# First turn of the attention heads in another order on four engines, and the forget gate's sums made one pair of products further back

## The chip, the cores and the metric

The program runs on one core of one Trainium2 chip. The metric is the device time of one execution in microseconds (us). A profiled execution gives a trace in which every instruction of every engine has its place; the times below are read from one such execution.

## The reference, cut to what matters

A decoder trunk of two layers works on 528 tokens (16 learned meta tokens and 512 of the input), 1024 channels, in float32. Layer 0 mixes tokens with eight stick-breaking heads and eight forgetting heads side by side. The change touches only that mixer:

```
proj  = h @ w_in                       # q, k, v of 8 stick-breaking and 8 forgetting heads, and 8 forget logits
log_f = log_sigmoid(f_logit + b_f);  c = cumsum(log_f)          # over the tokens
z   = qa @ ka.T * scale                # stick-breaking: weights from a reversed cumulative sum of log_sigmoid(-z)
a_w = exp(log_sigmoid(z) + rest);      out_sb  = a_w @ va
s   = qb @ kb.T * scale + c[q] - c[k]  # forgetting: causal softmax
out_fox = softmax(s) @ vb
h   = h + concat(out_sb, out_fox) @ w_out
```

The rest is RMS norms, four SwiGLU feed-forward halves (1024 to 2816 and back) and, in layer 1, a pooling mixer.

## The kernel before, in words

**Precision and products.** Every float32 operand is split into a high part (rounded by ScalarE, "hi") and a low part (the difference, made by VectorE, "lo"), and a product is three matmul passes: hi·hi, lo·hi, hi·lo. Large products are made two strips at a time, in *pairs*, with seven half-size block products in place of eight (a Strassen-like scheme). Each block product is 12 matmuls of 128x264. So each pair needs, on VectorE, sums of weight blocks (L2213, L2219, L2224), low parts of weights (`s23_low` L2240, `s14_low` L2245, `a_low` L2229, `a22_low` L2234) and four drains of results (L1338, L1345, L1352, L1359) with a scaling pass (L1365).

**The input projection.** 24 strips of 128 columns: four are made plainly, and 20 in ten pairs whose first strip `p.f` is 4, 6, ..., 22. Strips below `QK` = 16 are queries and keys; they are split and stored to DRAM (`qk_dram`), from which the heads are staged. Strips 16 to 23 are values and stay in SBUF (`v_rows`). The program of a pair on TensorE (`qkv_pe`) is: product 1; third product of the pair before; product 2; product 6 (waits for `s23_low` of this pair); fourth product of the pair before; product 7; product 5 (waits for `s14_low` of this pair). Then comes the next pair, whose first product waits for its `a_low`. In the last pair (`p.f` = 22) TensorE has extra work between: `first_turned_values` (transposes 0 and 1 of the values) ahead of product 6, and `first_scores` (scores of head step 0 and 1, transposes 2 and 3) ahead of product 7.

**Forget gate.** `fg`, `fg_abs`, `fg_sum`, `fg_one` are four rows of `fg_room`, which lies in the same SBUF as `q_all[0]` (three rows: the queries of head 0 of a pair of heads) and `fx_kk[0]` (the fourth row: forgetting keys). At the end of pair 16 VectorE makes the log-sigmoid (L1436) and its cumulative sum (a scan, L1438). ScalarE copies the high parts (L1195, L1196) in pair 18, VectorE makes the low parts at that pair's end (L1441, L1442; they raise `c_low`), GpSimd stores them to DRAM (L3294, raises `c_stored`), and they are read back as two small transfers of two rows into `fx_qc` and `fx_kc`.

**Staging (`stage_heads`, SyncE's DMA queue, a program written out by hand).** For the first head: four transfers of keys; wait for `c_low`; six of queries and forgetting queries into `q_all`, two of forgetting keys into `fx_kk`; wait for `c_stored`; two small ones of the sums; then `fetch_out(0..3)`, the first four strips of the output projection's weights (512 KB each, and each waits until the raw buffer is free). All fourteen transfers of head 0 count on one semaphore, `staged[0]`, and TensorE's first score (L885, `stick_scores(0, 0)`) waits for the whole of it. Later come head 1 and the values (L784, L788) into `head_v`.

**The heads' turns.** Eight steps (two heads of four tiles) per pair of heads, four pairs of heads. TensorE makes stick-breaking scores (L885, L891), forgetting scores (L903), sticks (L923, L927, L930), transposes of probabilities (L943), and values (L968 and on; L988). ScalarE makes |z|, exp, log (L1113, L1120, L1126), the softmax's exp (L1142), the softplus's high part (`act_split`, L1152) and the weights (L1161). VectorE masks (L1452), makes softplus (L1462), the running stick (L1477), the probabilities (L1514) and the low part of softplus (L1518, raises `sp_low`). GpSimd masks (L3307). The first turn (`hp` = 0) overlaps the end of the projection: value strips 22 and 23 are drained by `c21_out` and `bottom_scaled` (L1359, L1365) between steps, and eleven pieces of transposed values go out of PSUM (`v_turned_out`, L1155 on ScalarE, L731 on VectorE). In the first turn TensorE's forgetting scores of step 3 wait for `c21_out` of the last pair, transposes 8 and 9 for `bottom_scaled`, transpose 10 for copy 7, and the first product with values (`stick_values(0, 0)`, L968) for copy 9, for the GpSimd transfer of the first head's values (L3345, semaphore `v_first`), and for the zeroed half of `head_v[0]` (`v_zero`).

Of the kernel before, what the change touches and what calls it, by code (L numbers as in the profile page):

```python
# [30 lines left out]
ALU = mybir.AluOpType  # L31
AXX = mybir.AxisListType.X

P = 128
# [10 lines left out]
QKV, QKV_PLAIN = 24, 4  # L45
QK = 16
# [4 lines left out]
HD = 64  # L51
NH = 8
# [109 lines left out]
def trunk(nc, x, meta_tokens, g_ffn1, w_ffn1_in, w_ffn1_out, g_mix, g_ffn2, w_ffn2_in, w_ffn2_out,  # L162
# [5 lines left out]
    with ctx:  # L168
# [123 lines left out]

        fg, fg_abs, fg_sum, fg_one = (fg_room[0:NH, i, :] for i in range(4))
        fg_both, fg_low = fg_room[:, 0, :], fg_room[LOW_ROW:, 0, :]
# [449 lines left out]
        def stage_heads(sp, ph, fetch_out):  # L744
# [36 lines left out]
            def stage_v(hp, e, kinds, landed_v):  # L781
                for kind in kinds:
                    tiles = slice(0, QT - kind)
                    sp.dma_start(head_v[e][:, kind, tiles, HD * e:HD * (e + 1)],  # L784
                                 v_tok[:, kind, tiles, bass.ds((2 * hp + e) * HD, HD)]).then_inc(landed_v, 16)
                if e == 1 and 1 in kinds:
                    for a in range(2):
                        sp.dma_start(head_v[1][META * a:META * (a + 1), 1, QT - 1, HD * a:HD * (a + 1)],  # L788
                                     v_tok[0:META, 1, QT - 1, bass.ds((2 * hp + a) * HD, HD)]).then_inc(staged_v[e], 16)
# [4 lines left out]
            sp.wait_ge(aug_ones, 3)  # L794
            stage_keys(0, 0)
            sp.wait_ge(c_low, 2)
            stage_queries(0, 0)
            stage_forgetting(0, 0)
            sp.wait_ge(c_stored, 16)
            stage_sums(0, 0)  # L800
            for j in range(4):
                fetch_out(j)
            sp.wait_ge(p5_done, ph.pairs[-1].s + 1)
# [10 lines left out]
            sp.wait_ge(v_first, 16)  # L814
            sp.wait_ge(v_zero, 3)
            stage_v(0, 1, (0, 1), staged_v[1])
# [257 lines left out]
        def attn_act(act, ph, split, tail, root, a_high, s23_high, s14_high, a22_high, p1_copy, u2_copy, u4_copy, X, A):  # L1074
# [111 lines left out]
            for p in ph.pairs:  # L1186
# [3 lines left out]
                if prev is not None:  # L1190
                    p1_copy(ph, p, two)
                    s14_high(p, prev)
                    if prev.f == QK:
                        act.wait_ge(fg_step, 5)
                        nc.scalar.activation(c_parts[:, 0, :], fg_sum, ACT.Copy).then_inc(c_high, 1)  # L1195
                        nc.scalar.activation(c_parts[:, 2, :], fg_sum, ACT.Copy, scale=-1.0).then_inc(c_high, 1)  # L1196
                    top_high(prev)
                    if nxt is not None:
                        a_high(nxt)
                    else:  # L1200
                        nc.scalar.preload_act_table_set("natural_log_exp_and_others")
                        act.wait_ge(s14_lo, p.s + 1)
                        v_turned_out(act, 0, copy)
                    u2_copy(ph, p, two)
# [22 lines left out]
            def act_step(hp, g, first):  # L1227
# [3 lines left out]
                if first and g == 2:  # L1231
                    act_log(hp, 2)
                    act_probs(hp, 2)
                    v_turned_out(act, 6, copy)
                    act_split(hp, 2)
                    v_turned_out(act, 7, copy)
                    return
# [48 lines left out]
        def attn_dve(dve, ph, split, tail, inverse, clear_sums, weight_sums_13, weight_sum_2, weight_sum_4, a_low, a22_low,  # L1286
# [111 lines left out]
            for p in ph.pairs:  # L1398
# [17 lines left out]
                if prev is not None:  # L1416
                    s14_low(p)
                    if prev.f < QK:
                        qk_low(prev.f)
                if prev is not None and nxt is not None:  # L1420
                    a_low(nxt)
# [9 lines left out]
                if nxt is not None:  # L1431
                    a22_low(nxt)
                if p.f == QK:
                    dve.wait_ge(fg_act, 3)
# [3 lines left out]
                    nc.vector.tensor_tensor_scan(fg_sum, fg_one, fg, 0.0, ALU.mult, ALU.add).then_inc(fg_step, 1)  # L1438
                elif p.f == QK + 2:
                    dve.wait_ge(c_high, 2)  # L1440
                    nc.vector.tensor_tensor(c_parts[:, 1, :], fg_sum, c_parts[:, 0, :], ALU.subtract).then_inc(c_low, 1)  # L1441
                    nc.vector.tensor_tensor(c_parts[:, 3, :], c_parts[:, 0, :], fg_sum, ALU.subtract).then_inc(c_low, 1)  # L1442

# [36 lines left out]
            def dve_step(hp, g, first):  # L1480
# [3 lines left out]
                if first and g == 2:  # L1484
                    dve_mask(hp, 2)
                    dve_softplus(hp, 2)
                    c21_out(last_p)
                    bottom_scaled(last_p)
# [1753 lines left out]
        def _(pool):  # L3242
# [14 lines left out]
            for ph in PHASES:  # L3257
# [81 lines left out]
                weight_mask(0, 0)  # L3339
                weight_mask(0, 1)  # L3340
                wait_v_copy(pool, 3)
                wait_v_copy(pool, QT - 1)
                pool.wait_ge(v_first, 16)
                pool.wait_ge(unit_done, ph.n0 + QKV)
                pool.dma_start(head_v[0][:, 0, 0:QT, 0:HD], v_tok[:, 0, 0:QT, 0:HD]).then_inc(v_first, 16)  # L3345
                softplus_mask(0, 2)
                for e in range(2):
                    nc.gpsimd.memset(head_v[e][:, :, :, HD * (1 - e):HD * (2 - e)], 0.0).then_inc(v_zero, 1)
                    pool.wait_ge(v_zero, e + 1)
                nc.gpsimd.memset(head_v[1][:, 1, QT - 1, HD:2 * HD], 0.0).then_inc(v_zero, 1)  # L3350
# [53 lines left out]
```

## Time and profile before

| | us |
|---|---|
| median of 3 runs (lowest, highest) | 1757.29 (1756.66, 1757.46) |
| the profiled execution's own time | 1756.96 |
| its span in the trace | 1755.2 |
| TensorE busy | 1739.5 (99%) |
| VectorE busy | 1401.1 (80%) |
| ScalarE busy | 939.0 (53%) |
| GpSimd busy | 71.8 (4%) |
| granted TensorE clock | 1.0 of full speed throughout |

The span is the stretch from the first to the last instruction; the execution's own time is 1.8 us longer. Times in the rows count from the span's start. The input projection's pairs lie at about 390 to 510 us, the first turn of the heads at 498 to 529 us, the other three turns up to 616 us.

### The profile page before, as it was taken

The page shows a single profiled execution, that of the slowest core. Times are in us where ns is not written, and L with a number is a line of the kernel's source. Part 1 is how long each engine was busy: PE and PEld are TensorE (multiplying, and loading weights), DVE is VectorE, ACT ScalarE, POOL GpSimd, SP SyncE. Part 2 cuts the span into 40 slices and gives each one's busy share as a digit, 9 for nine tenths or more (in the row PEclk, how much of TensorE's full clock was granted, in tenths as well). Part 3 has the DMA queues.
Part 4 walks back from the last instruction along what each step waited for, and adds up shares of the span by engine and source line. Part 5 has one row for each costly group of instructions (what it writes and reads, how often), then busy time and mean ns, then how long its engine had stood idle before and what let it go on. Part 6 is the DMA issues. An engine that isn't in the chain of part 4 may idle for free.

```text
span 1755.2 us, 34355 instructions
## 1 busy us (share of the span) xinstructions
PE 1739.5 (99%) x13600; PEld 1693.1 (96%) x13600; DVE 1401.1 (80%) x2018; ACT 939.0 (53%) x1554; POOL 71.8 (4%) x193
## 2 busy tenths in 40 slices
PE   8999999999999999999999999999999999999998
PEld 8999999999998899999999999999999988899997
DVE  6856998789988858848998688489987788499875
ACT  6433655555578844625655546246555445266555
POOL 0000000002122202000000000000000000000000
PEclk9999999999999999999999999999999999999999
DMA  5243333236655332333343323333342323343332
GB/s 159 85 121 97 97 108 110 80 103 197 196 157 149 88 109 85 97 97 97 97 119 92 102 87 108 97 96 97 97 113 74 91 77 104 89 114 110 97 95 74
DMA packets 334087, 187.01 MB, mean 107 GB/s; under 512 B 17713, under 2 KB 324593, under 8 KB 333937
## 3 DMA queue, kind: packets, MB, share of 16 engines
q1 hardware_dynamic: 330144, 175.31, 35.6%
q0 software_dynamic: 2960, 8.98, 1.4%
q8 instruction: 106, 1.74, 0.4%
q10 hardware_dynamic: 832, 0.62, 0.1%
q14 instruction: 45, 0.36, 0.1%
HBM read 171.58 MB, written 10.88 MB: 104 GB/s over the span
## 4 chain that ended last, share of the span: by engine, by line
PE 88%; DVE 8%; issue 2%; ACT 1%; DMA 1%; POOL 0%; DVEq 0%; ACTq 0%; SPq 0%; POOLq 0%
PE pair L2820 50%; PE pair L2792 18%; PE pair L2761 8%; PE pair L3156 4%; PE pair L2807 1%; PE pair L968 1%; PE pair L988 1%; PE pair L3032 1%; PE pair L2998 1%; DVE sums_w L2213 1%; DVE w_lo L2245 1%; DVE w_lo L2240 1%; DVE qk_lo L1319 1%; PE pair L903 0%; PE pair L885 0%
## 5 line engine op out<-in xcount | busy, mean ns | idle before, releaser
L2820 PE MATMUL pair<-b_hi,w_hi 128*128 128x264 f32 (+1 forms) x1464 | 415.9, 284 | 0.0
L2820 PE MATMUL pair<-b_lo,w_hi 128*128 128x264 f32 (+1 forms) x1464 | 415.0, 283 | 0.0
L2820 PE MATMUL pair<-b_hi,w_lo 128*128 128x264 f32 (+1 forms) x1464 | 414.6, 283 | 0.0
L2820 PEld LDWEIGHTS pair<-b_hi,w_hi 128*128 128x128 f32 x1464 | 275.7, 188 | 0.9 <-issue 0.5
L2820 PEld LDWEIGHTS pair<-b_hi,w_lo 128*128 128x128 f32 x1464 | 275.7, 188 | 0.0
L2820 PEld LDWEIGHTS pair<-b_lo,w_hi 128*128 128x128 f32 x1464 | 275.6, 188 | 0.0
L1738 ACT ACTIVATE w_hi<-sums_w 128x1024 fp32r<-128x1024 f32 x188 | 198.6, 1057 | 104.7 <-PE pair L2820 60.9
L1738 ACT ACTIVATE w_hi<-raw_all 128x1024 fp32r<-128x1024 f32 (+1 forms) x188 | 158.9, 845 | 141.9 <-PE pair L2820 101.2
L2820 PE MATMUL pair<-blocks_hi,w_hi 128*128 128x264 f32 (+1 forms) x816 | 231.3, 283 | 0.3 <-ACT parts L1925 0.3
L2820 PE MATMUL pair<-blocks_lo,w_hi 128*128 128x264 f32 (+1 forms) x816 | 231.5, 284 | 0.0
L2820 PE MATMUL pair<-blocks_hi,w_lo 128*128 128x264 f32 (+1 forms) x816 | 230.8, 283 | 0.0
L2792 PE MATMUL pair<-b_hi,w_lo 128*128 128x264 f32 (+1 forms) x766 | 173.8, 298 | 0.0
L2792 PE MATMUL pair<-b_hi,w_hi 128*128 128x264 f32 (+1 forms) x766 | 173.5, 298 | 0.0
L2792 PE MATMUL pair<-b_lo,w_hi 128*128 128x264 f32 (+1 forms) x766 | 173.4, 298 | 0.0
L2131 DVE TENSOR_TENSOR w_lo<-raw_all,w_hi 128x1024 fp32r<-128x1024 f32 x117 | 142.6, 1221 | 28.2 <-ACT w_hi L1709 28.2
L1709 ACT ACTIVATE w_hi<-raw_all 128x1024 fp32r<-128x1024 f32 x117 | 121.7, 1050 | 63.3 <-PE pair L2792 58.8
L2820 PEld LDWEIGHTS pair<-blocks_hi,w_hi 128*128 128x128 f32 x816 | 153.8, 188 | 0.7 <-ACT parts L1925 0.5
L2820 PEld LDWEIGHTS pair<-blocks_hi,w_lo 128*128 128x128 f32 x816 | 153.7, 188 | 0.0
L2820 PEld LDWEIGHTS pair<-blocks_lo,w_hi 128*128 128x128 f32 x816 | 153.5, 188 | 0.2
L2240 DVE TENSOR_TENSOR w_lo<-sums_w,w_hi 128x1024 fp32r<-128x1024 f32 x94 | 114.8, 1221 | 24.0 <-ACT w_hi L1738 24.0
L2637 DVE SCALAR_TENSOR_TENSOR h<-pair,h 128x528 f32<-128x528 f32 (+1 forms) x61 | 42.9, 703 | 109.0 <-PE pair L2792 108.4
L2245 DVE TENSOR_TENSOR w_lo<-sums_w,w_hi 128x1024 fp32r<-128x1024 f32 x94 | 114.6, 1219 | 17.8 <-ACT w_hi L1738 17.6
(355 smaller groups left out, 3788.1 us busy)
## 6 DMA issues: line engine op xcount, KB each, us to landing
raw_all<-in_w_ffn_in SPq DMA_DIRECT2D x173, 512.0 KB, 4.0
raw_all<-in_w_ffn_out SPq DMA_DIRECT2D x64, 512.0 KB, 4.4
raw_all<-in_w_ffn_out SPq DMA_DIRECT2D x32, 384.0 KB, 3.7
raw_all<-in_w_attn_in SPq DMA_DIRECT2D x24, 512.0 KB, 4.7
q_all<-qk_dram SPq DMA_DIRECT2D x48, 132.0 KB
qk_dram<-qk_hi POOLq DMA_DIRECT2D x16, 264.0 KB, 4.5
qk_dram<-qk_lo POOLq DMA_DIRECT2D x16, 264.0 KB, 3.0
raw_all<-in_w_attn_out SPq DMA_DIRECT2D x8, 512.0 KB, 4.9
```

The costliest lines, as they stand in the source:

```text
L968: mm = nc.tensor.matmul(o_main[:, 0, q0 - META:SEQ], head_v[e][:, 0, 3 - s, :], w[:, 0:nq], start=(g == 0), stop=True, skip_group_check=True)
L988: mm = nc.tensor.matmul(own, head_v[e][:, 1, b, :], turned_p[s][:, b, :], start=(g == 0 and b == 0), stop=True, skip_group_check=True)
L1709: nc.scalar.activation(w_hi[j][:, :], raw[j][:, :], ACT.Copy).then_inc(hi_ready, 1)
L1738: return nc.scalar.activation(dst, src, ACT.Copy)
L2131: nc.vector.tensor_tensor(w_lo[j][:, :], raw[j][:, :], w_hi[j][:, :], ALU.subtract).then_inc(lo_ready, 1)
L2240: nc.vector.tensor_tensor(w_lo[1][:, :], S23, w_hi[1][:, :], ALU.subtract).then_inc(s23_lo, 1)
L2245: nc.vector.tensor_tensor(w_lo[2][:, :], s14(p.q), w_hi[2][:, :], ALU.subtract).then_inc(s14_lo, 1)
L2637: nc.vector.scalar_tensor_tensor(hm, pair_of(OUT_BANK[m], ph.last), 0.5, hm, ALU.mult, ALU.add).then_inc(drained, 1)
L2761: mm = nc.tensor.matmul(psum[j][:, bank, c0:c0 + cols], w[j][:, blk], rhs[v][:, k, t0:t0 + cols], start=(k == 0 and w is w_hi and v == 0), ...
L2792: mm = nc.tensor.matmul(bank_of[:, bank, c0:c0 + cols], w[slot][:, blk], rhs[v][:, k, from_:from_ + cols], start=(k == 0 and w is w_hi and ...
L2820: mm = nc.tensor.matmul(dst, w[slot][:, c0 + kk * P:c0 + (kk + 1) * P], rhs(v, kk), start=(fresh and kk == 0 and w is w_hi and v == 0), st ...
L3156: mm = nc.tensor.matmul(psum[j][:, bank, c0:c0 + cols], w[j][:, blk], X[v][:, k, t0:t0 + cols], start=(k == 0 and w is w_hi and v == 0), s ...
```

## The change

It moves work; no arithmetic is added or removed.

- Forget gate: log-sigmoid and scan move from the end of pair 16 to the end of pair 18, the high parts on ScalarE from pair 18 to pair 20, the low parts on VectorE from the end of pair 18 to the middle of pair 20, after `s14_low` and ahead of `a_low` of the last pair. `fg_sum` changes places with `fg_one`, so that it lies under `fx_kk[0]`.
- SyncE's queue: queries and forgetting queries wait for the scan only (`fg_step` 5), forgetting keys for `c_low`; `fetch_out(0..3)` comes ahead of the sums. The wait for `v_zero` 3 stands only ahead of the two small transfers of meta values.
- VectorE: in step 2 of the first turn `c21_out` comes ahead of `softplus`.
- ScalarE: in step 2 copy 7 comes ahead of `act_split`.
- GpSimd: `head_v[0]` is zeroed first, then the mask of step 2's softplus, then the transfer of the first head's values; `head_v[1]` is zeroed only once `sp_low` is 3, that is after VectorE's L1518 of step 2.

```diff
-        fg, fg_abs, fg_sum, fg_one = (fg_room[0:NH, i, :] for i in range(4))
+        fg, fg_abs, fg_one, fg_sum = (fg_room[0:NH, i, :] for i in range(4))
...
                 if e == 1 and 1 in kinds:
+                    if isinstance(hp, int) and hp == 0:
+                        sp.wait_ge(v_zero, 3)
                     for a in range(2):
...
             stage_keys(0, 0)
+            sp.wait_ge(fg_step, 5)
+            stage_queries(0, 0)
+            put(0, fx_qq[0][0:HD, :], part(0, 0, 8))
+            put(0, fx_qq[0][HD:P, :], part(0, 1, 8))
             sp.wait_ge(c_low, 2)
-            stage_queries(0, 0)
-            stage_forgetting(0, 0)
+            put(0, fx_kk[0][0:HD, :], part(0, 0, 12))
+            put(0, fx_kk[0][HD:P, :], part(0, 0, 12))
+            for j in range(4):
+                fetch_out(j)
             sp.wait_ge(c_stored, 16)
             stage_sums(0, 0)
-            for j in range(4):
-                fetch_out(j)
...
             sp.wait_ge(v_first, 16)
-            sp.wait_ge(v_zero, 3)
             stage_v(0, 1, (0, 1), staged_v[1])
...
-                    if prev.f == QK:
+                    if prev.f == QK + 2:
                         act.wait_ge(fg_step, 5)
...
                     v_turned_out(act, 6, copy)
+                    v_turned_out(act, 7, copy)
                     act_split(hp, 2)
-                    v_turned_out(act, 7, copy)
...
                     s14_low(p)
                     if prev.f < QK:
                         qk_low(prev.f)
+                    if p.f == QK + 4:
+                        dve.wait_ge(c_high, 2)
+                        (the two low parts, c_low)
...
-                if p.f == QK:
+                if p.f == QK + 2:
                     (log-sigmoid and scan)
-                elif p.f == QK + 2:
-                    (the two low parts, c_low)
...
                     dve_mask(hp, 2)
+                    c21_out(last_p)
                     dve_softplus(hp, 2)
-                    c21_out(last_p)
                     bottom_scaled(last_p)
...
                 weight_mask(0, 1)
+                pool.wait_ge(unit_done, ph.n0 + QKV)
+                nc.gpsimd.memset(head_v[0][:, :, :, HD:2 * HD], 0.0).then_inc(v_zero, 1)
+                pool.wait_ge(v_zero, 1)
+                softplus_mask(0, 2)
                 wait_v_copy(pool, 3)
                 wait_v_copy(pool, QT - 1)
                 pool.wait_ge(v_first, 16)
-                pool.wait_ge(unit_done, ph.n0 + QKV)
                 pool.dma_start(head_v[0][:, 0, 0:QT, 0:HD], v_tok[:, 0, 0:QT, 0:HD]).then_inc(v_first, 16)
-                softplus_mask(0, 2)
-                for e in range(2):
-                    nc.gpsimd.memset(head_v[e][:, :, :, HD * (1 - e):HD * (2 - e)], 0.0).then_inc(v_zero, 1)
-                    pool.wait_ge(v_zero, e + 1)
+                pool.wait_ge(sp_low, 3)
+                nc.gpsimd.memset(head_v[1][:, :, :, 0:HD], 0.0).then_inc(v_zero, 1)
+                pool.wait_ge(v_zero, 2)
```

## Rows read from the trace of the kernel before

**Rows 1.** The page: busy time of each engine, share of the span, instructions.
```profile
PE 1739.5 (99%) x13600; PEld 1693.1 (96%) x13600; DVE 1401.1 (80%) x2018; ACT 939.0 (53%) x1554; POOL 71.8 (4%) x193
```
**Rows 2.** Timeline of TensorE in the last pairs (start, length, line, idle before and releaser).
```profile
473.02 0.51 PE L2820 MATMUL pair<-qkv_t,w_hi 128*128 128x264 f32 x2 [0.44 <-DVE w_lo L2240]
...
477.98 0.53 PE L2820 MATMUL pair<-qkv_t,w_hi 128*128 128x264 f32 x2 [0.32 <-DVE w_lo L2245]
...
489.75 0.28 PE L2820 MATMUL pair<-b_hi,w_hi 128*128 128x264 f32 x1
...
494.14 1.03 PE L872 MATMUL pair<-ident,v_rows 128*128 128x128 f32 x8
...
497.92 0.34 PE L885 MATMUL pair<-q_all,sb_kk 128*128 128x144 f32 x2
```
**Rows 3.** Timeline of VectorE, pairs 16 to 20.
```profile
469.88 0.69 DVE L1436 SCALAR_TENSOR_TENSOR fg_room<-fg_room 8x528 f32<-8x528 f32 x1
470.61 1.25 DVE L1438 TENSOR_TENSOR_SCAN fg_room<-fg_room 8x528 f32<-8x528 f32 x1
...
481.75 0.69 DVE L1442 TENSOR_TENSOR c_room<-c_room,fg_room 8x528 fp32r<-8x528 f32 x1
...
487.83 1.22 DVE L2229 TENSOR_TENSOR w_lo<-raw_all,w_hi 128x1024 fp32r<-128x1024 f32 x1
```
**Rows 4.** Timeline of SyncE's DMA queue, head 0 and the weights behind it.
```profile
482.47 3.97 SPq L747 DMA_DIRECT2D q_all<-qk_dram  x6
486.48 1.24 SPq L747 DMA_DIRECT2D fx_kk<-qk_dram  x2
...
488.55 4.82 SPq L1621 DMA_DIRECT2D raw_all<-in_w_attn_out  x4
```
**Rows 5.** The tile raw_all from 486 to 500 us: the four weight transfers.
```profile
L1621 SPq DMA_DIRECT2D raw_all<-in_w_attn_out x4: 393/537/1604, 488.5 to 491.8; - x4
...
DMA to landing us min/median/max: 5.0/6.1/6.9
```
**Rows 6.** Busy time by stretch (PE, PEld, DVE, ACT, POOL, clock, DMA share, GB/s).
```profile
497.00:498.00 1.00, 1.00 (x11) 1.00 (x10) 0.00 (x0) 0.06 (x1) 0.00 (x0) 1.00 0.24 70
```
**Rows 7.** Timeline of TensorE at the end of the projection.
```profile
509.40 0.28 PE L2820 MATMUL pair<-qkv_t,w_lo 128*128 128x264 f32 x1
...
510.55 0.45 PE L903 MATMUL pair<-fx_kk,q_all 128*128 128x400 f32 x1 [0.41 <-DVE v_rows L1359]
...
511.56 0.85 PE L872 MATMUL pair<-ident,v_rows 128*128 128x128 f32 x6 [0.20 <-DVE v_rows L1365]
512.68 0.66 PE L872 MATMUL pair<-ident,v_rows 128*128 128x128 f32 x4 [0.28 <-ACT v_tok L1155]
...
514.77 0.48 PE L968 MATMUL pair<-b_rows,head_v 128*128 128x144 f32 x2 [0.28 <-ACT v_tok L1155]
```
**Rows 8.** Timeline of VectorE, step 2 of the first turn.
```profile
509.58 0.57 DVE L1462 SCALAR_TENSOR_TENSOR b_rows<-pair,b_rows 128x400 f32<-128x400 f32 x1 [0.56 <-ACT b_rows L1126]
510.07 0.42 DVE L1359 TENSOR_TENSOR v_rows<-pair,qkv_parts 128x264 f32<-128x264 f32 x1
...
511.76 0.84 DVE L1514 TENSOR_SCALAR b_rows<-b_rows,stats 128x400 f32<-128x400 f32 x1
```
**Rows 9.** Timeline of GpSimd there, and the landing of its transfer (line L3345).
```profile
510.35 0.90 POOL L3345 DMA_DIRECT2D head_v<-v_tok  x1 [2.86 <-DVE b_rows L1462]
511.26 0.54 POOL L3307 TENSOR_SCALAR_AFFINE_SELECT b_rows<-b_rows 128x128 f32<-128x128 f32 x1
...
DMA to landing us min/median/max: 3.9/3.9/3.9
```
**Rows 10.** Timeline of ScalarE there.
```profile
512.27 0.36 ACT L1155 ACTIVATE v_tok<-pair 16x256 f32<-16x256 f32 x1
```
**Rows 11.** DMA issues of the page: transfers like GpSimd's, by SyncE, and the smallest.
```profile
head_v<-v_tok SPq DMA_DIRECT2D x7, 160.0 KB, 2.5
...
head_v<-v_tok SPq DMA_DIRECT2D x8, 4.0 KB, 1.7
```

More of the change, by code:

```diff
@@ L1419, in attn_dve @@
                         qk_low(prev.f)
+                    if p.f == QK + 4:
+                        dve.wait_ge(c_high, 2)
+                        nc.vector.tensor_tensor(c_parts[:, 1, :], fg_sum, c_parts[:, 0, :],
+                                                ALU.subtract).then_inc(c_low, 1)
+                        nc.vector.tensor_tensor(c_parts[:, 3, :], c_parts[:, 0, :], fg_sum,
+                                                ALU.subtract).then_inc(c_low, 1)
                 if prev is not None and nxt is not None:
@@ L1438, in attn_dve @@
                     nc.vector.tensor_tensor_scan(fg_sum, fg_one, fg, 0.0, ALU.mult, ALU.add).then_inc(fg_step, 1)
-                elif p.f == QK + 2:
-                    dve.wait_ge(c_high, 2)
-                    nc.vector.tensor_tensor(c_parts[:, 1, :], fg_sum, c_parts[:, 0, :], ALU.subtract).then_inc(c_low, 1)
-                    nc.vector.tensor_tensor(c_parts[:, 3, :], c_parts[:, 0, :], fg_sum, ALU.subtract).then_inc(c_low, 1)
             def dve_mask(hp, g):
```

## Prediction, made before the changed kernel was run

> **What bounds the kernel now.** The page's first part comes first: TensorE is busy for 99% of the span, no other engine above 80% [rows 1]. So only time in which TensorE stands still can be won, and every delay of TensorE is paid in full. Next I read TensorE's own timeline around the forget gate and the first turn, looking for the few brackets with idle time, and for matmuls that start later than their pitch (the 12 matmuls of a product take 1.46 us where nothing is awaited). There are two places. In pair 18, products 6 and 5 each wait for VectorE's low parts. Between their starts lie 36 matmuls, which take 4.39 us unhindered (489.75 to 494.14) and took 4.96 here, so the second wait cost 0.57, 0.25 more than its bracket, which counts from a modelled end; some 0.1 of that is the restart itself. For the first, 0.44 in its bracket, I take 0.6 and for the second 0.5 [rows 2]. Behind the projection come four more: 0.41, 0.20, 0.28 and 0.28 us [rows 7]. From 515 us on TensorE has almost no gap until the heads are done, so a shift made before that point reaches the end. All that stands still here is 1.1 + 1.17 = 2.3 us, or 0.13% of the time; a measurement of this kernel can tell 0.2% (3.5 us) from no change. That alone says "within 0.2%" unless a new wait comes in.
>
> **Part 1, the forget gate's sums.** On VectorE the same instructions run between 469.88 and the end of pair 20, without idle time in either order. Before, log-sigmoid and scan (469.88 to 471.78, 1.90 us) stand ahead of pair 18's low parts [rows 3]. After, these come 1.90 us earlier: neither 0.6 nor 0.5 is left. TensorE runs 1.1 us ahead. But scan and low parts (two of 0.69, pitch 0.62) [rows 3] now all lie in pair 20 and just before it, ahead of `a_low` of the last pair. The list ahead of that `a_low` is the same as before, so it still ends at 487.83 + 1.22 = 489.05 [rows 3]. TensorE would want it at 489.75 - 1.1 = 488.65 [rows 2] and gets it at about 489.10. A new stall of 0.45 us takes part back: **-0.65 us** is left at this point. Low parts of the last pair's product 6 end where they did, and TensorE needs them only behind transposes 0 and 1 (494.14) [rows 2]; ScalarE's two copies go into gaps. Both cost nothing; without these gaps they would cost their 1.2 us.
>
> **Part 2, SyncE's queue.** TensorE would now reach the first score at 497.92 - 0.65 = 497.27 [rows 2]. Before, it found all fourteen transfers landed. After, `c_low` comes at 487.9 instead of 482.44 (its L1442 ended there) [rows 3], as the low parts now end where `a_low` starts. The six transfers that no longer wait for it gain nothing, since they were early. The two of forgetting keys go out at 487.9 instead of 486.48, the first weights at 487.9 + 1.24 = 489.15 instead of 488.55 [rows 4]: +0.6. The third and fourth weights still wait for the last pair's low parts (the fourth goes out at 491.8) [rows 5]. The two small transfers of sums now follow all four, issued at about 494. The last weight lands 6.9 us after its issue, at 491.8 + 6.9 = 498.7 [rows 5], and the DMA engines are down to a share of 0.24 at 497 to 498 [rows 6], so most of its parts are in by then. The stream is saturated, so it ends 0.6 later: most engines at 497.8 or so, the slowest at 499.3. The sums come behind. No row shows what a two-row transfer behind 2 MB costs; the bounds are 497.3 (it overtakes, nothing is awaited) and 499.3 + 0.1. I take 498.4, nearer to the traffic's end than to the slowest part, because two rows don't touch every engine. That is 1.15 us of new stall, and the first score starts **0.5 us later** than before. The four weights themselves are needed only at 616 us: nothing. The store of the sums (L3294) goes out at 488.6 and is in long before 494: nothing.
>
> The Trainium skill ("DMA: Bandwidth & Descriptors", "Queues, rings and completion order") speaks against this order: on each DMA engine descriptors are taken in ring order, and the semaphore's write lands only after every earlier write of that engine. The same page ("Why a DMA increments its semaphore by 16 and not by 1") puts a transfer with two outer rows on the two lowest-numbered engines. By that rule the sums can't overtake and don't meet the slow engines either; it would give the value I take, and the overtaking case would fall out. No row here settles it.
>
> **Part 3, step 2 of the first turn** (times of before; all of it moves with the 0.5). The fourth product ends at 509.40 + 0.28 = 509.68 [rows 7]. `c21_out` can start then instead of at 510.07 [rows 8] and the scores behind it start 0.35 earlier than 510.55 [rows 7]. But `bottom_scaled` still has `c21_out` and softplus ahead of it: 509.72 + 0.35 + 0.49 = 510.56, as against 510.53, so transpose 8 stays at 511.6: the gain is waited away. Transpose 10 waited for copy 7, which ended at 512.27 + 0.36 = 512.63 [rows 10]; it now goes ahead of the split at 510.6, so the 0.28 stall and its slack (0.37 together) go. VectorE's L1514 took 0.84 us instead of the 0.43 of its like, beside GpSimd's memsets [rows 8]; with `head_v[1]` zeroed later, this is won too, so sticks and transposes of step 2 keep pace. TensorE could start the first product with values at 514.77 - 0.65 = 514.1.
>
> It then meets GpSimd's transfer. That went out at 510.35 and landed 3.9 later, 514.25, just under cover [rows 9]. Now zeroing `head_v[0]` (0.7 from 509.7) and the mask come ahead of it. Softplus ends at 510.65, the mask lasts 510.75 to 511.3 (0.54) [rows 9], so the transfer goes out at 511.3 to 511.6. It lands at 511.45 + 3.9 = 515.35; with 2.5, what SyncE's queue takes for the same size [rows 11], at 513.9, which is no wait at all. I take 515.2, near the row of this very transfer, since the DMA engines are as full as before and SyncE's value transfers now go out beside it. That is **+0.5 us** against 514.77. The mask is 0.5 earlier and ScalarE's exp and log with it; that is no help while the transfer is late.
>
> The Trainium skill ("SBUF — State Buffer", "SBUF: two separate sides") says that GpSimd can't write a DMA's descriptors while VectorE runs a two-port operation, and L1514 now lies beside just this issue. By that rule up to one L1514 comes on top of 515.2. The 0.84 agrees that the two engines get in each other's way; whether a descriptor write does so, no row shows.
>
> **Sum.** Projection -0.65; staging +1.15; step 2 +0.5: +1.0 us. The profiled execution took 1756.96, which gives 1757.96; the median of the runs is 0.33 above it, so I forecast 1758.3.
>
> **The rivals.**
> (a) *Only one of the two transfers is late.* If the sums land by 497.3: -0.65 + 0.5, time 1757.1. If GpSimd's transfer lands by 514.1: +0.5 - 0.65, the same 1757.1. For it: the bounds above; against it: a saturated stream and 3.9 us. Chance 0.28.
> (b) *Neither is late, faster.* -0.65 - 0.65 = -1.3: 1756.0. The small transfers would have to overtake 2 MB. Chance 0.17. Faster by over 0.2% would need more standstill than the trace has: 0.03 for what I overlook.
> (c) *Slower: the sums are the bound, far out.* The fourth weight took 1.6 us to issue, as the row's longest [rows 5]; the queue may be full, and SyncE might get the sums out only as weights leave it. They would then start when the slowest part is in, 499.3, and take a small transfer's own 1.7 [rows 11]: 501.0, that is +3.1, with step 2 +3.6 in all: 1760.9. It decides from a landing after 497.9 on; at 500.9 it passes 0.2%. For it: the 1.6. Against: a full queue still lets a transfer in before the last has landed. Chance 0.05.
> (d) *The change doesn't do what it says:* a pair later the scan hits `s23_low` of pair 20 (by my count ready at 482.4, needed at 482.7), and the stalls only move. Then -0.1 in place of -0.65 up to 489, but TensorE waits for the sums anyway: 1758.3 again. Chance 0.1, mostly inside the forecast.
>
> **How the numbers follow.** My own case, both late (with d): 0.47; its own range is 1757.3 to 1759.8 (sums 498.0 to 499.4, values 514.8 to 515.8). The range takes in (a) and (b): from 1756.0, less 0.4 of run-to-run spread, to 1759.8 with 0.2 more. Within 0.2%: everything but 0.03 faster and 0.04 slower.
>
> **What would show it.** Right: no idle ahead of L2820 near 473 and 478; a short one at the first product of pair 22; one of over 1 us ahead of the first L885, released by a DMA into `fx_qc` or `fx_kc`; none ahead of transpose 10; the first L968 waiting for a DMA into `head_v`, not for ScalarE; L1514 back to 0.43. Wrong: the first L885 at 497.3 without idle time, or the first L968 about 17.0 us or less behind it (16.85 before).

## Result and the profile after

The changed kernel takes 1761.25 us (median of 9 runs, 1758.21 to 1765.45) against 1757.59 (9 runs, 1756.66 to 1758.02): a ratio of 1.0024, 95% interval 1.0016 to 1.0032. The forecast was 1758.3 in a range of 1755.6 to 1760.0. The change makes the kernel slower by a quarter of a percent, beyond that range, and its runs spread over 7.2 us where the kernel before spreads over 1.4. The profiled execution took 1761.35 us, span 1759.5.

The timeline of TensorE in the changed kernel, against [rows 2] and [rows 7] (start, length, line, idle before and releaser):

```profile
489.36 0.39 PE L2827 MATMUL pair<-b_hi,w_hi 128*128 128x264 f32 x1 [0.32 <-DVE w_lo L2236]
...
499.57 0.42 PE L890 MATMUL pair<-q_all,sb_kk 128*128 128x144 f32 x2 [1.78 <-DMA fx_kc<-c_dram]
...
502.68 0.42 PE L2827 MATMUL pair<-qkv_t,w_lo 128*128 128x264 f32 x1
502.90 0.64 PE L2827 MATMUL pair<-qkv_t,w_hi 128*128 128x264 f32 x2
503.34 0.42 PE L2827 MATMUL pair<-qkv_t,w_lo 128*128 128x264 f32 x1
...
515.01 1.28 PE L877 MATMUL pair<-ident,v_rows 128*128 128x128 f32 x10 [0.71 <-DVE v_rows L1370]
519.23 0.51 PE L973 MATMUL pair<-b_rows,head_v 128*128 128x144 f32 x2 [1.78 <-DMA head_v<-v_tok]
```

The two waits of pair 18 are gone, as forecast. In their place stand two long waits for transfers, 1.78 us each. Between them is a thing that no row of before had. Three matmuls of 128x264 take 0.66 us from start to start (502.68 to 503.34), where they take 0.36 elsewhere. The busy time by stretch says why (PE, PEld, DVE, ACT, POOL, granted clock, DMA share, GB/s):

```profile
495.00:500.00 5.00, 3.22 (x28) 3.04 (x27) 2.19 (x4) 1.03 (x3) 0.53 (x1) 1.00 0.86 213
500.00:505.00 5.00, 5.00 (x31) 5.00 (x31) 3.62 (x17) 4.27 (x15) 1.33 (x5) 0.66 0.00 0
505.00:510.00 5.00, 5.00 (x45) 4.92 (x44) 2.10 (x7) 1.82 (x5) 1.98 (x6) 1.00 0.34 94
```

0.66 over 5 us is 3.4 us at half: TensorE's clock was granted at 1.2 GHz instead of 2.4 for 3.4 us, beginning about 2 us after TensorE had gone on (between 501.5 and 502, where it had gone on at 499.57). In the kernel before the clock is at 1.0 in all these stretches.

VectorE and SyncE's queue, against [rows 3] and [rows 4]:

```profile
480.24 1.25 DVE L1449 TENSOR_TENSOR_SCAN fg_room<-fg_room 8x528 f32<-8x528 f32 x1
...
487.48 0.69 DVE L1429 TENSOR_TENSOR c_room<-c_room,fg_room 8x528 fp32r<-8x528 f32 x1
488.10 1.21 DVE L2236 TENSOR_TENSOR w_lo<-raw_all,w_hi 128x1024 fp32r<-128x1024 f32 x1
```

```profile
481.51 3.66 SPq L747 DMA_DIRECT2D q_all<-qk_dram  x6
488.20 1.10 SPq L747 DMA_DIRECT2D fx_kk<-qk_dram  x2
489.35 4.68 SPq L1628 DMA_DIRECT2D raw_all<-in_w_attn_out  x4
494.08 1.58 SPq L747 DMA_DIRECT2D fx_qc<-c_dram  x1
495.70 0.26 SPq L747 DMA_DIRECT2D fx_kc<-c_dram  x1
```

Up to the weights the queue does what the prediction says, 0.25 us later, because this execution's start took that much longer (VectorE's chain begins 0.25 later too). The first transfer of the sums is not as forecast: it took 1.58 us to issue, where it took 0.44 before, so the sums were out at 496.0 and not 1.1 us earlier. The four weights, against [rows 5]:

```profile
L1628 SPq DMA_DIRECT2D raw_all<-in_w_attn_out x4: 581/768/1559, 489.4 to 492.5; - x4
...
DMA to landing us min/median/max: 4.9/6.7/7.7
```

The last part of the last weight lands at 492.5 + 7.7 = 500.2, as against 498.7 before: 1.5 later (1.25 without the later start), not 0.6. GpSimd's timeline in step 2, against [rows 9]:

```profile
513.03 0.64 POOL L3349 MEMSET head_v<- 128x640 f32 x1 [2.27 <-PE pair L2827]
514.08 0.67 POOL L3314 TENSOR_SCALAR_AFFINE_SELECT b_rows<-b_rows 128x128 f32<-128x128 f32 x1 [0.41 <-DVE b_rows L1469]
514.70 0.90 POOL L3355 DMA_DIRECT2D head_v<-v_tok  x1
```

SyncE's transfers of the other values start at 514.85, right beside GpSimd's; before, they started at 512.71, 2.4 us behind it. The landing of GpSimd's transfer, from the row of that line, and VectorE's timeline beside it, against [rows 8]:

```profile
DMA to landing us min/median/max: 4.5/4.5/4.5
```

```profile
513.01 0.43 DVE L1364 TENSOR_TENSOR v_rows<-pair,qkv_parts 128x264 f32<-128x264 f32 x1 [0.70 <-PE pair L2827]
...
515.15 0.62 DVE L1521 TENSOR_SCALAR b_rows<-b_rows,stats 128x400 f32<-128x400 f32 x1
```

**Where the 4.4 us went.** The first product with values starts at 519.23 instead of 514.77, 4.46 later, and nothing changes that behind it. Step by step: start of the execution +0.25; first product of pair 22 at 489.36 instead of 489.75, so -0.64 for the projection; without a wait the first score would come at 497.92 + 0.25 - 0.64 = 497.53 and comes at 499.57, +2.04; from there to transpose 8 it is 515.01 - 499.57 = 15.44 against 511.56 - 497.92 = 13.64, +1.80, nearly all of it the clock (in e3, e9 and e10 below, with the same fall, this distance grows by 1.67 to 1.73; the other 0.1 is the wait ahead of transpose 8, 0.71 here and 0.55 there); from transpose 8 to the first values 4.22 against 3.21, +1.01. Sum +4.46.

### The profile page after: what moved, and what is told of

It reads as the page before. It is cut to its first block, busy times and chain, and to the rows that moved or that the text cites. A ratio compares the mean times of both kernels' runs of the same rounds, so it can differ in the third digit from the quotient of the medians.

```text
span 1759.5 us, 34353 instructions
## 1 busy us (share of the span) xinstructions
PE 1741.1 (99%) x13600; PEld 1695.1 (96%) x13600; DVE 1400.4 (80%) x2018; ACT 939.6 (53%) x1554; POOL 71.8 (4%) x193
## 3 DMA queue, kind: packets, MB, share of 16 engines
q8 instruction: 105, 1.72, 0.4%
## 4 chain that ended last, share of the span: by engine, by line
PE 91%; DVE 5%; issue 2%; ACT 1%; DMA 1%; SPq 0%; POOL 0%; DVEq 0%; ACTq 0%; POOLq 0%
PE pair L2827 53%; PE pair L2799 18%; PE pair L2768 8%; PE pair L3163 4%; PE pair L2814 1%; PE pair L973 1%; PE pair L993 1%; PE pair L3039 1%; PE pair L3005 1%; PE pair L908 0%; PE pair L890 0%; PE pair L928 0%; PE pair L3093 0%; DVE rinv L2163 0%; DMA x_in<-in_x 0%
```

## Experiments

Every run is timed against the kernel before on the same chip. The kernel before itself measured 1756.74 beside e1 to e4, 1757.05 beside e5 to e7 and e9, and 1757.25 beside e8, e10, e12 and e14, so runs of different groups are best compared by their difference from it. "Distance" below is the time from one start to another in the same trace, which takes the start of the execution out.

**Sums ahead of the weights again (e1).** The changed kernel with this edit:

```diff
+            sp.wait_ge(c_stored, 16)
+            stage_sums(0, 0)
             for j in range(4):
                 fetch_out(j)
-            sp.wait_ge(c_stored, 16)
-            stage_sums(0, 0)
```

> The changed kernel with the two transfers of sums ahead of the four weights again. In the changed kernel's trace TensorE stands still for about 2 us ahead of the first score, and after it the granted clock is at 1.2 GHz for 3.4 us. Theory CLOCK: the second follows from the first, so both go: no idle time ahead of the first L890, clock 1.0 there; the wait ahead of the first product with values (1.78 us, for GpSimd's transfer) stays. 1761.25 - 2.0 - 1.7 = 1757.5. Rival WAIT ALONE: the clock falls for another reason (the amount of DMA traffic, or the heads' small matmuls): it falls here too, and 1759.3 is left. A third possibility: the wait for GpSimd's transfer makes the clock fall by itself: then a fall shows at 519 us and the time is 1758 to 1759.5.

1756.60 us (1755.25 to 1759.60) against 1756.74: ratio 0.9998 [0.9989, 1.0007]. The wait at the first score and the clock's fall behind it are gone together. But the profiled execution (1758.62) shows the third possibility too: the wait for GpSimd's transfer is 2.39 us, and the clock falls behind that one. Not every execution can be like it. Its way from the first score to the first values is 18.47 us, 2.03 more than the 16.44 of e4 below. The fastest of e4's runs took 1754.86, so with this wait, and without any fall, no run of e1 should lie below 1756.9. Six of the eleven do (1755.25 to 1756.60). The wait must be shorter in those; no trace shows one.

```profile
515.20 0.51 PE L973 MATMUL pair<-b_rows,head_v 128*128 128x144 f32 x2 [2.39 <-DMA head_v<-v_tok]
```

```profile
500.00:505.00 5.00, 5.00 (x46) 4.92 (x44) 3.48 (x14) 3.27 (x11) 2.60 (x6) 1.00 0.37 106
...
515.00:520.00 5.00, 4.80 (x20) 3.79 (x21) 1.67 (x7) 1.79 (x5) 0.52 (x3) 0.67 0.35 95
```

**Weights ahead, alone on the kernel before (e2).**

```diff
-            sp.wait_ge(c_stored, 16)
-            stage_sums(0, 0)
             for j in range(4):
                 fetch_out(j)
+            sp.wait_ge(c_stored, 16)
+            stage_sums(0, 0)
```

> The kernel before with one edit: fetch_out(0..3) ahead of the sums. The weights go out when they did, the sums at 493.4, behind them. QUEUE theory (the sums can't overtake the weights): they land at about 498, between most engines' last parts; the first score starts at 498.1 to 498.8 instead of 497.92; no clock fall, because the wait is under 1 us; 1757.6 to 1758.5. Rival OVERTAKE: no wait, 1757.6.

1757.30 against 1756.74, ratio 1.0002 [0.9993, 1.0011]. No wait at all:

```profile
487.70 5.47 SPq L1621 DMA_DIRECT2D raw_all<-in_w_attn_out  x4
493.22 0.44 SPq L747 DMA_DIRECT2D fx_qc<-c_dram  x1
```

```profile
497.93 0.34 PE L885 MATMUL pair<-q_all,sb_kk 128*128 128x144 f32 x2
```

The weights leave 0.85 earlier than in the kernel before (487.70, not 488.55), since the sums are out of their way, and the sums have landed by 497.9, ahead of the slowest part of the last weight (started at 491.65, landed 6.6 later, 498.25). So the order in the queue costs nothing by itself. It costs in company with the gate's move, which makes the forgetting keys and all that is behind them start at 488.2. This run does not decide between queueing and overtaking: it shows only that the sums need not wait for every part of the weights.

**GpSimd's order of before (e3).** The changed kernel with its block of before in `pool`: transfer, mask of step 2, both memsets.

> The changed kernel with GpSimd's order of before (transfer of the first head's values first, then the mask of step 2, then both memsets). The wait of 1.78 us at the first product with values goes down to 0.3 or so; VectorE's L1521 of step 2 takes 0.84 again. The wait for the sums and the clock at 1.2 GHz after it stay. If nothing else hangs on GpSimd's order: 1761.25 - 1.2 = 1760.0, still with a spread of several us from run to run. If the spread of the changed kernel comes from the second wait (the clock falling there in some executions), the spread is gone here and all runs lie near 1760.

1759.16 (1757.66 to 1759.96), ratio 1.0012 [1.0003, 1.0021]. The wait for the sums is the same, the other one is 0.29, and the spread shrinks from 7.2 to 2.3 us. The expected 0.84 us of L1521 did not come: it took 0.43 (see e8).

```profile
499.39 0.42 PE L890 MATMUL pair<-q_all,sb_kk 128*128 128x144 f32 x2 [1.80 <-DMA fx_kc<-c_dram]
...
517.43 0.51 PE L973 MATMUL pair<-b_rows,head_v 128*128 128x144 f32 x2 [0.29 <-DMA head_v<-v_tok]
```

```profile
500.00:505.00 5.00, 5.00 (x30) 5.00 (x30) 3.78 (x17) 4.28 (x15) 1.34 (x5) 0.66 0.00 0
```

The distance from the first score to the first values is 18.04, 1.60 more than in e4 below; the clock's fall behind the sums' wait is in it. The changed kernel's slowness thus has two sources. Most of the scatter goes with the second wait: e1, which keeps only that one, spreads over 4.4 us.

**Both undone (e4).** The edits of e1 and e3 together.

> The changed kernel with the sums ahead of the weights and GpSimd's order of before: what is left is the forget gate a pair further back, the queries' early fetch, copy 7 ahead of the split, and c21_out ahead of softplus. Projection -0.65, transpose 10's wait gone -0.3: 1757.6 - 0.9 = 1756.7, clock 1.0 throughout, spread under 1.5 us. If the forget gate's move is what harms: above 1758.

1755.36 (1754.86 to 1756.74) against 1756.74, ratio 0.9993 [0.9984, 1.0002]; clock at 1.0. It is 1.4 us faster than the kernel before, where 0.9 was expected. It lies 3.8 us below e3 (the sums' wait of 2.0 and its clock fall) and 1.2 below e1 (GpSimd's wait, with a fall in some executions). The two costs add up: taken from the kernel before beside each, the medians are +3.66 for the changed kernel, +2.42 for e3, -0.14 for e1 and -1.38 for e4, and 3.80 + 1.24 = 5.04 is just what lies between the first and the last.

```profile
488.37 0.39 PE L2827 MATMUL pair<-b_hi,w_hi 128*128 128x264 f32 x1 [0.20 <-DVE w_lo L2236]
...
496.65 0.34 PE L890 MATMUL pair<-q_all,sb_kk 128*128 128x144 f32 x2
...
510.29 1.28 PE L877 MATMUL pair<-ident,v_rows 128*128 128x128 f32 x10 [0.55 <-DVE v_rows L1370]
513.09 0.51 PE L973 MATMUL pair<-b_rows,head_v 128*128 128x144 f32 x2 [0.36 <-DMA head_v<-v_tok]
```

**The gate's move alone (e5).** e4 with step 2 of VectorE, ScalarE and SyncE as before too.

> The kernel before with the forget gate's move and what hangs on it alone: gate a pair further back, fg_sum under fx_kk, queries fetched early; the sums ahead of the weights, and step 2 of all engines in the order of before. If the gate's move is worth what TensorE's idle time in pair 18 says, less the new wait at pair 22: first score 0.65 us earlier, time 0.65 below the kernel before of the same chip, 1756.1. If step 2's new order on VectorE and ScalarE adds to that in the run before (e4_both, 1755.4), this run lies about 0.4 above it.

1756.35 against 1757.05, ratio 0.9997 [0.9988, 1.0006]: 0.7 lower, the size of the -0.65, though the interval alone can't tell it from nothing. It lies 0.7 above e4, where 0.4 was expected from step 2's order. Its trace has the new wait at pair 22 (0.27) and step 2's four waits of before, unchanged:

```profile
489.17 0.39 PE L2826 MATMUL pair<-b_hi,w_hi 128*128 128x264 f32 x1 [0.27 <-DVE w_lo L2235]
...
514.30 0.48 PE L972 MATMUL pair<-b_rows,head_v 128*128 128x144 f32 x2 [0.28 <-ACT v_tok L1159]
```

**Step 2's order alone (e6).** The kernel before with the edits of step 2 on the four engines.

> The kernel before with step 2's new order on VectorE, ScalarE, GpSimd and the moved wait for v_zero on SyncE's queue, nothing else. GpSimd's transfer goes out about 1.2 us later and TensorE waits for it 1.8 to 2.4 us ahead of the first product with values. Theory CLOCK: a wait of that length lets the granted clock fall to 1.2 GHz for 3.4 us in most executions: 1756.7 + 0.6 + up to 1.7 = 1757.3 to 1759, with a spread of over 2 us. Rival WAIT ALONE: 1757.3, spread as in the kernel before.

1756.76 against 1757.05, ratio 1.0001 [0.9992, 1.0010], with runs from 1755.38 to 1759.74. Seven of the eleven lie at or below 1757.3, four at 1758.9 to 1759.7. So the time is that of the kernel before, below the 1757.3 to 1759 expected. The profiled execution (1758.93) is one of the four: a wait of 1.72 and the fall behind it. The lower seven can't differ from it by the fall alone. From the first score to the first values it took 17.80 us, 0.95 more than the 16.85 before. The fastest of the runs of the kernel before took 1756.21, so with this wait and no fall none should lie below 1757.2, and six do; and the middles of the two groups (1756.4 and 1759.3) are 2.9 us apart, more than one fall's 1.7. The wait too must be shorter in the lower group. No trace shows that; over the traces of all runs GpSimd's transfer took between 3.7 (e12) and 4.9 us (e1) to land.

```profile
515.25 0.51 PE L969 MATMUL pair<-b_rows,head_v 128*128 128x144 f32 x2 [1.72 <-DMA head_v<-v_tok]
```

```profile
515.00:520.00 5.00, 4.75 (x21) 3.71 (x22) 2.35 (x9) 2.16 (x6) 1.11 (x5) 0.70 0.37 95
```

**Sums between the second and third weight (e7).** e4 with

```diff
-            sp.wait_ge(c_stored, 16)
-            stage_sums(0, 0)
-            for j in range(4):
+            for j in range(2):
                 fetch_out(j)
+            sp.wait_ge(c_stored, 16)
+            stage_sums(0, 0)
+            for j in range(2, 4):
+                fetch_out(j)
```

> e4_both with the two transfers of sums between the second and the third weight, so that they follow 1 MB instead of none (e4) or 2 MB (the changed kernel). QUEUE theory: they land behind the second weight, at about 495.5 to 496.2, just ahead of the first score (496.7): no wait, 1755.4 as e4_both. If a small transfer behind the weights is held up for another reason (SyncE's queue full until all are out), TensorE waits over 1 us here too and the time is 1758.

1756.09 against 1757.05, ratio 0.9994 [0.9985, 1.0003]. No wait at the first score: its distance from the first product of pair 22 is 496.30 - 488.03 = 8.27, as in e4 (8.28). So with the gate moved, 1 MB ahead of the sums is free and 2 MB is not; a queue with 1 MB in it holds nothing up (the first transfer of the sums took 0.25 us to issue). Whether the 1.58 us that it took behind 2 MB made the sums late, or the weights' own traffic did, was not tried. The profiled execution also shows the shortest wait with a fall behind it, 1.00 us, though GpSimd's order is that of before: the transfer took 4.6 us to land, against 4.0 in e4.

```profile
513.38 0.51 PE L975 MATMUL pair<-b_rows,head_v 128*128 128x144 f32 x2 [1.00 <-DMA head_v<-v_tok]
```

```profile
515.00:520.00 5.00, 5.00 (x24) 3.91 (x23) 2.87 (x11) 2.91 (x11) 1.28 (x5) 0.66 0.42 117
```

**A pure standstill (e9, e10).** e4 with one wait ahead of TensorE's first score, for the landing of the second weight (e9) or the third (e10); nothing else moves. A standstill is time in which TensorE does nothing.

```diff
+                land_wait(pe, ph.n0 + QKV + 1, 1)     # e10: + 2, 2
                 stick_scores(0, 0)
                 fox_scores(0, 0)
```

> e4_both with one wait more: TensorE waits ahead of its first score until the second of the four weights has landed. No work is added and no transfer moved, so this is a pure standstill of some length (landing at about 498.2, demand at 496.65: 1.2 to 1.8 us). WAIT ALONE: the time rises by the standstill only, 1755.4 + 1.5 = 1756.9. CLOCK: it rises by the standstill and by what 3.4 us at 1.2 GHz cost (1.7): 1758.6, and the trace has the granted clock at 0.5 about 1.5 us after TensorE starts again. If the standstill needed is longer than 1.5 us, no fall shows; that brackets it.

> As e9_hold_w1, but TensorE waits for the third weight: a standstill of about 3.5 us instead of about 2. e9 read 1758.5 for 1755.4 (+3.1, of which the standstill is some 2). CLOCK, with a fall of fixed length: +3.5 and once more about 1.3 to 1.7, so 1760.3 to 1760.6, one stretch of 3.4 us at 1.2 GHz. Rival: a longer standstill lowers the clock for longer (two such stretches): 1762.

e9 takes 1758.54, ratio 1.0009 [1.0000, 1.0018]; e10 takes 1762.24, ratio 1.0030 [1.0018, 1.0043]. The standstill itself, by the distance from the first product of pair 22 to the first score less 8.28, is 498.46 - 488.48 - 8.28 = 1.70 in e9 and 501.20 - 489.54 - 8.28 = 3.38 in e10. First e9's first score and its fall, then the same of e10:

```profile
498.46 0.42 PE L890 MATMUL pair<-q_all,sb_kk 128*128 128x144 f32 x2 [1.55 <-DMA raw_all<-in_w_attn_out]
```

```profile
500.00:505.00 5.00, 5.00 (x31) 5.00 (x30) 3.67 (x16) 3.55 (x13) 1.34 (x5) 0.67 0.07 19
```

```profile
501.20 0.42 PE L890 MATMUL pair<-q_all,sb_kk 128*128 128x144 f32 x2 [3.24 <-DMA raw_all<-in_w_attn_out]
```

```profile
500.00:505.00 5.00, 3.80 (x21) 3.83 (x22) 1.20 (x7) 2.95 (x11) 0.52 (x3) 0.71 0.28 70
505.00:510.00 5.00, 5.00 (x42) 4.92 (x41) 3.75 (x13) 3.12 (x8) 1.94 (x5) 0.95 0.10 24
```

Against e4's 1755.36, e9 is 3.2 slower (2.9, when each is taken from the kernel before beside it): 1.7 of standstill and 1.2 to 1.5 on top. No work was added and the transfers are the same (the four weights start at 491.5 to 494.5 in e4 and at 491.7 to 494.4 in e9, and take up to 7.4 and 7.3 us to land), so the clock's fall follows from the standstill and not from the traffic: WAIT ALONE, which would give 1757.1, is out.

e10 is 6.9 slower than e4 (6.4 by the kernel before): 3.4 of standstill and 3.0 to 3.5 on top, about twice as much. Its profiled execution, the fastest of the six at 1761.02, has only one stretch of 3.4 us at 1.2 GHz, and there the way from the first score to the first values is 18.18 us, 1.74 more than e4's 16.44: one fall. Where the other runs lose the rest stays open. A second stretch, the rival, would fit the median, but the mean clocks (0.999, 0.997, 0.997, 0.999, 0.997, 0.998 from the fastest to the slowest) don't follow the times, and no trace shows it.

**head_v[1] zeroed later, GpSimd's transfer still first (e8).**

```diff
                 softplus_mask(0, 2)
-                for e in range(2):
-                    nc.gpsimd.memset(head_v[e][:, :, :, HD * (1 - e):HD * (2 - e)], 0.0).then_inc(v_zero, 1)
-                    pool.wait_ge(v_zero, e + 1)
+                nc.gpsimd.memset(head_v[0][:, :, :, HD:2 * HD], 0.0).then_inc(v_zero, 1)
+                pool.wait_ge(v_zero, 1)
+                pool.wait_ge(sp_low, 3)
+                nc.gpsimd.memset(head_v[1][:, :, :, 0:HD], 0.0).then_inc(v_zero, 1)
+                pool.wait_ge(v_zero, 2)
```

> e4_both with head_v[1] zeroed only behind VectorE's L1525 of step 2, as the changed kernel does, but GpSimd's transfer and the mask still first. VectorE's tensor_scalar of step 2 (L1521) goes from about 0.84 to 0.43 us. If TensorE's way to the first product with values hung on it, that start comes up to 0.3 us earlier against the first score; if GpSimd's transfer is the bound there (0.36 us idle, released by a DMA, in e4_both), nothing changes: 1755.4 and the same distance of 16.44 us.

1755.89, ratio 0.9993 [0.9984, 1.0002]: the same as e4. Nothing was left to win: L1521 takes 0.43 in e4 already, where it starts at 510.71 and GpSimd's memsets at 510.23. It takes 0.84 where both start at the same time (both at 511.16 in e12, both at 511.76 in the kernel before).

**c21_out behind softplus (e12).** e4 with the order of before on VectorE.

> e4_both with c21_out behind softplus again. The prediction says that the earlier scores of step 3 are waited away at transpose 8. Then: idle 0.4 ahead of the scores of step 3 and 0.2 ahead of transpose 8, in place of 0.55 ahead of transpose 8 alone; transpose 8 starts at the same distance from the first score (13.64 us in e4_both) within 0.1, and the time stays at 1755.4. If the swap is worth something, transpose 8 comes 0.3 to 0.4 later.

1755.97, ratio 0.9994 [0.9985, 1.0003]. The prediction's reading holds to the hundredth: transpose 8 starts 510.96 - 497.32 = 13.64 behind the first score in both.

```profile
509.95 0.45 PE L908 MATMUL pair<-fx_kk,q_all 128*128 128x400 f32 x1 [0.41 <-DVE v_rows L1364]
510.96 1.28 PE L877 MATMUL pair<-ident,v_rows 128*128 128x128 f32 x10 [0.20 <-DVE v_rows L1370]
513.91 0.48 PE L973 MATMUL pair<-b_rows,head_v 128*128 128x144 f32 x2 [0.52 <-ACT v_tok L1160]
```

From transpose 8 to the values it is 2.95, against 2.80 in e4 and 3.21 in the kernel before: copy 7 ahead of the split is worth 0.26, the swap 0.15.

**Low parts behind a_low (e14).** e4 with the two low parts of the gate's sums moved down by one instruction group, behind `a_low(nxt)` of the last pair.

> e4_both with the low parts of the gate's sums (c_low) behind a_low of the last pair, not ahead of it. The wait that the move puts ahead of the first product of pair 22 (0.2 to 0.5 us) goes, and the first score comes 0.4 us earlier: 1755.0. The forgetting keys and the sums are staged 1.2 us later; should they then land behind TensorE's first score (e4 has some 2 us to spare), a wait shows there instead and the time is 1755.4 or more.

1755.04 (1754.47 to 1756.43) against 1757.25, ratio 0.9989 [0.9980, 0.9998]. The wait at pair 22 is gone, the first score comes at 496.06, and nothing waits for the sums. It is the fastest version, and the only one whose interval lies below 1. It is 2.2 below the kernel before beside it, e4 1.4; the two intervals overlap, so between them it is too near to tell.

```profile
485.94 1.22 DVE L2236 TENSOR_TENSOR w_lo<-raw_all,w_hi 128x1024 fp32r<-128x1024 f32 x1
...
487.70 0.69 DVE L1431 TENSOR_TENSOR c_room<-c_room,fg_room 8x528 fp32r<-8x528 f32 x1
```

## Why the prediction was wrong, point by point

- **What bounds the kernel**: the step that failed. "Every delay of TensorE is paid in full" took a wait at its own length, and from the small total of standstill I concluded "within 0.2% unless a new wait comes in". Two new waits did come in, as I said they would, and a wait can cost more than its length: about 1.7 us more each time the clock falls behind it. I looked at the granted clock of the kernel before, saw 1.0 everywhere, and had no term for it. In the profiled execution that term is about 1.7 of the 4.46 us. Without it that execution would have come to 1759.7, inside the range. The rest over the forecast +1.0 is sizes: the sums' wait 0.9, GpSimd's 0.5, the start of the execution 0.25 and the wait ahead of transpose 8 0.1.
- **Part 1** was right in mechanism and size, and rival (d) did not happen, as the two waits of pair 18 are gone and no other stands in their place before pair 22: -0.65 forecast, -0.64 found, with the new wait at the first product of pair 22 (0.32 in its bracket). e5 has it by itself. That the wait is avoidable, e14 shows.
- **Part 2** was right in mechanism, wrong in size. I took 498.4 for the sums' landing, near the end of the traffic, with the slowest part at 499.3. TensorE was let go at 499.57, 0.25 of which is the late start: +2.04 in place of +1.15. The stream's end was 1.25 later beside the late start, where I had only moved the issue by 0.6, and the sums left SyncE 1.1 us later than a free queue would have let them, as the first took 1.58 us to issue and not 0.44. The trace shows the forgetting keys, GpSimd's store of the sums and the first weights setting out within 1.2 us (488.20 to 489.35; before, the store was out at 483.1); that they slow each other is my reading, not tested. By the Trainium skill ("DMA: Bandwidth & Descriptors", "Queues, rings and completion order") the sums can't overtake the weights of their engines; the trace fits that, as TensorE is let go at 499.57, after most of the stream, and ahead of its slowest part at 500.2, but it does not show the engines one by one.
- **Part 3**: transpose 8 gains nothing (right, e12). GpSimd's transfer is late (right) and leaves when forecast: at 514.70, or 511.25 in times of before (3.45 less, by transpose 8). But it took 4.5 us to land, not 3.9, and I had rounded 515.35 down to 515.2: +1.01 in place of +0.5. The range had one row for the landing; over all the traces it is 3.7 to 4.9. That SyncE's transfers of values now start beside GpSimd's (514.85, not 2.4 us behind it) may have added to it; with 1.2 us between them, in e4, it landed in 4.0. This was not tried by itself.
- **The rule on descriptors** of the Trainium skill ("SBUF — State Buffer", "SBUF: two separate sides") did not bite as weighed: GpSimd's issue took 0.90 in both kernels. VectorE's L1521 beside it took 0.62 instead of 0.43 (so it did in e1 and e6). The section gives the shared ports to whichever of the two starts first, and makes the other wait; the trace agrees on the order, as the issue started at 514.70 and L1521 at 515.15, so the loser of the two was VectorE.
- **Rivals.** (a) and (b), under 1757.2, are what e4, e7 and e14 come to with the late transfers mended. (c) had the right sign and, within 0.4 us, the right time by luck: the queue was not held until the weights were in, and the clock, which (c) leaves out, makes up its time. The first of the sums did take 1.58 us to issue, but it was out at 495.7, with the last weights landing until 500.2.
- **The range** had only sums of waits in it. With one fall of the clock behind each of the two waits it would have reached 1760.0 + 3.4 = 1763.4.

## What to carry to other kernels

Where the clock is at its full level throughout, a new wait of TensorE for a transfer (they were 1.0 to 2.4 here) should be priced at its length plus a chance of 1.7 us, and a change that trades several stalls of 0.3 to 0.6 us for one of 1.8 us can lose at the same total: none of the short ones here was followed by a fall. Before work is moved back by one stage, look at what is queued behind its last result: here a late semaphore put 2 MB of weights in the same microseconds as a transfer of two rows that TensorE needed next. And where runs of a changed kernel scatter more than before, read the granted clock of each run first, and don't take the one profiled execution for all of them.

## What the runs showed that was not expected

- The clock fell to 1.2 GHz behind waits with brackets of 1.00, 1.55, 1.72, 1.78, 1.80, 2.39 and 3.24 us (e7, e9, e6, the changed kernel, e3, e1, e10), for 3.4 us each time, beginning 0.9 (e10) to 2.3 us (e7) after TensorE had gone on; it did not fall behind the 0.2 to 0.56 us of e4, e8, e9, e12 and e14, nor behind the 0.71 of the changed kernel. It does not fall behind every longer one: in the changed kernel's profiled execution the 1.78 us ahead of L973 left it at 1.0. What decides in one execution was not tried.
- The Trainium skill ("TensorE: Matmul & The Clock Gate", "Part 1: The HAM clock gate") has the clock at its low level after idleness and at its high level after sustained work; the trace agrees, 0.66 granted in the 5 us behind the wait and 1.00 from then on.
- The mean granted clock of the changed kernel's nine runs goes from 0.999 (1758.21 us) to 0.996 (1765.45 us). A mean lower by 0.003 over 1760 us is 5.3 us of the clock lost, an estimate that makes up most of the 7.2 between them. One stretch of 3.4 us at half is 1.7, or 0.001 of the mean. The mean also counts a fall at the end of the execution, where TensorE has no more work (0.85 from 1750 to 1755 us in the kernel before), so with one fall in it it reads 0.999 in some profiled executions and 0.998 in others, and the estimate is good to a third.
